# One fused transformer kernel: the last two weight chunks of each projection taken together, and convolution taps on 32x32 tiles of the matrix engine

## The reference, cut to what matters

```
mix = y @ w_out            # or: mix = act(conv(h @ w_up)) @ w_down
x = x + rmsnorm(mix, post_gain)
h = rmsnorm(x, pre_gain)   # input of the next half layer
```

```
u = h @ w_in + b_in                       # 1024 -> 2048
u = u[..., :D] * sigmoid(u[..., D:])
u = causal_dwconv(u, dw, dw_b)            # per channel: 31 taps over tokens
u = silu(layer_norm(u, ln_g, ln_b))
y = u @ w_out + b_out
```

## Time and profile before

| | us |
|---|---|
| median of 3 runs | 3412.98 |
| lowest, highest | 3412.93, 3414.3 |
| the profiled execution, its device time | 3412.23 |
| its span, first to last instruction | 3410.4 |
| PE busy | 3254.4 (95%) |
| DVE busy | 1780.0 (52%) |
| ACT busy | 1237.5 (36%) |
| POOL busy | 136.8 (4%) |

### The profile page before, as it was taken

The page is one execution under the profiler, slowest core; times in us unless marked ns, Lnnn a source line. Parts: engine busy times, 40 slices in busy tenths (PEclk is TensorE's granted clock), DMA queues, the critical chain, the costliest instruction groups (busy, mean ns, idle before and its releaser), DMA issues.

```text
span 3410.4 us, 41633 instructions
## 1 busy us (share of the span) xinstructions
PE 3254.4 (95%) x16677; PEld 2660.3 (78%) x16677; DVE 1780.0 (52%) x2348; ACT 1237.5 (36%) x1676; POOL 136.8 (4%) x148
## 2 busy tenths in 40 slices
PE   8899999999999899999999988999899999999999
PEld 7566888888877588888887657888788888888887
DVE  4655445553465734555527956553434424555543
ACT  3544224443334622444324234442322212243432
POOL 1130000000020300000000010000000000000000
PEclk9999999999999999999999999999999999999999
DMA  6221322322341123223232112223231221223322
GB/s 162 47 72 50 99 93 92 98 92 93 93 104 55 36 88 98 87 99 98 93 104 64 60 44 91 94 92 105 68 106 59 65 87 62 75 81 98 98 86 87
DMA packets 231696, 288.16 MB, mean 84 GB/s; under 512 B 5397, under 2 KB 188717, under 8 KB 231565
## 3 DMA queue, kind: packets, MB, share of 16 engines
q1 hardware_dynamic: 225628, 266.89, 24.2%
q0 software_dynamic: 5936, 19.40, 2.6%
HBM read 284.18 MB, written 2.10 MB: 84 GB/s over the span
## 4 chain that ended last, share of the span: by engine, by line
PE 86%; DVE 8%; ACT 3%; issue 3%; POOL 0%; DMA 0%; DVEq 0%; ACTq 0%; POOLq 0%
PE ps L1437 18%; PE ps L1439 18%; PE ps L1438 18%; PE ps L1553 6%; PE ps L1554 6%; PE ps L1555 6%; PE ps L1474 2%; PE ps L1476 2%; PE ps L1475 2%; PE ps L1813 2%; PE ps L1622 1%; ACT t_whi L588 1%; PE ps L1658 1%; DVE t_wlo L925 1%; PE ps L1907 1%
## 5 line engine op out<-in xcount | busy, mean ns | idle before, releaser
L925 DVE TENSOR_TENSOR t_wlo<-t_wraw,t_whi 128x2048 fp32r<-128x2048 f32 x252 | 582.4, 2311 | 1349.3 <-ACT t_whi L588 1349.3
L588 ACT ACTIVATE t_whi<-t_wraw 128x2048 fp32r<-128x2048 f32 x252 | 482.7, 1916 | 1498.3 <-PE ps L1439 1009.4
L1437 PE MATMUL ps<-t_hh,t_whi 128*128 128x512 f32 (+1 forms) x2640 | 988.9, 375 | 34.2 <-DVE t_hl L995 25.6
L1439 PE MATMUL ps<-t_hh,t_wlo 128*128 128x512 f32 (+1 forms) x2640 | 980.6, 371 | 0.0
L1438 PE MATMUL ps<-t_hl,t_whi 128*128 128x512 f32 (+1 forms) x2640 | 980.4, 371 | 0.0
L1437 PEld LDWEIGHTS ps<-t_hh,t_whi 128*128 128x128 f32 x2640 | 501.9, 190 | 125.9 <-issue 23.7
L1438 PEld LDWEIGHTS ps<-t_hl,t_whi 128*128 128x128 f32 x2640 | 501.7, 190 | 86.7 <-issue 2.9
L1439 PEld LDWEIGHTS ps<-t_hh,t_wlo 128*128 128x128 f32 x2640 | 501.5, 190 | 84.4
L1555 PE MATMUL ps<-t_whi,t_midl 128*128 128x512 f32 x704 | 273.9, 389 | 0.0
L1553 PE MATMUL ps<-t_whi,t_midh 128*128 128x512 f32 x704 | 273.9, 389 | 0.0
L1554 PE MATMUL ps<-t_wlo,t_midh 128*128 128x512 f32 x704 | 273.9, 389 | 0.0
(11 more groups left out here) (258 smaller groups left out, 3971.4 us busy)
## 6 DMA issues: line engine op xcount, KB each, us to landing
t_wraw<-in_w_in_dram SPq DMA_DIRECT2D x46, 1024.0 KB, 5.3
t_wraw<-in_w_up_dram SPq DMA_DIRECT2D x44, 1024.0 KB, 5.1
t_wraw<-in_ffn_w_in_dram SPq DMA_DIRECT2D x44, 1024.0 KB, 5.1
t_wraw<-in_w_kv_dram SPq DMA_DIRECT2D x24, 1024.0 KB, 5.2
t_wraw<-in_w_down_dram SPq DMA_DIRECT2D x20, 1024.0 KB, 5.0
t_wraw<-in_ffn_w_out_dram SPq DMA_DIRECT2D x20, 1024.0 KB, 5.0
t_wraw<-in_w_branch_dram SPq DMA_DIRECT2D x12, 1024.0 KB, 5.0
t_wraw<-in_w_q_dram SPq DMA_DIRECT2D x12, 1024.0 KB, 5.1
```

The source lines that it names most:

```text
L588: sc.activation(whi[slot][:, :], wraw[slot][:, :], ACT.Copy).then_inc(w_hi, 1)
L925: v.tensor_tensor(wlo[slot][:, :], wraw[slot][:, :], whi[slot][:, :].bitcast(F32), ALU.subtract).then_inc(w_lo, 1)
L1437: te.matmul(out, wh, xh, start=first, stop=False)
L1439: return te.matmul(out, wl, xh, start=False, stop=last)
```

## The change

Three things change.

**Last two chunks together** (`last_two`). PE takes tiles 0 and 1 of the last but one chunk, then tiles 0 and 1 of the last (complete now), then tiles 2 and 3 of the last but one, which frees that chunk; then it turns row 0, does tile 2 of the last chunk, turns row 1, does tile 3. So rows 0 and 1 are turned within the product and no longer in `first_two`. In the hand-over the preparation of the next stage's first chunk (`hi(c - 1)`, `lo(c - 1)`) stands after the first two rows, that of its second chunk (`hi(c)`, `lo(c)`) after `add_mix` of row 3. The table load for the square root moves ahead of the squares of the first half.

**First two chunks**: the second chunk's half for tiles 0 and 1 is split into its two row tiles, with both transposes (rows 2 and 3) between them. After down2 the list of its own only loses its first two transposes.

**Convolution taps**: DVE does 15 taps of tiles 0 to 5 and 11 of tiles 6 and 7; PE does the other 16 and 20. PE is used as 16 tiles of 32x32: row group i holds channels 32i to 32i+31, column group g takes taps g, g+4, ... and writes partitions 32g of bank i (`partial_taps`). ACT copies the four banks to `part` (`copy_partials`), PE adds the four groups with a stacked 128x32 identity (`join_taps`), DVE adds the result (`add_joined`). POOL makes the 32x32 diagonals and sums tiles 0 to 6 of `vb` into `usum`, so that PE needs two matmuls for the layer norm's mean.

```diff
-PE_TAPS = 10
+DVE_TAPS = (15, 15, 15, 11)
...
-            tapd = sb("tapd", 4 * PE_TAPS * P, stack=s)
+            tapd = [sb(f"tapd{i}", 20 * 32, stack=s) for i in range(2)]
+            part, usum, stack = sb("part", 8 * T, stack=s), sb("usum", T, stack=s), sb("stack", 32, stack=s)
...
+        def pe_taps(t):
+
+            return TAPS - DVE_TAPS[t // 2]
+
+        def part_bank(t, i):
+
+            return bank(4 + i) if t < KT - 1 else bank(i)
...
+            def tap_diagonals(t):
+
+                n = pe_taps(t)
+                if t >= 2:
+                    pool.wait_ge(tapped, t - 1)
+                r0 = ROWS["cm_dw_2"][0] + 8 * DVE_TAPS[t // 2] + t
+                w = pvec[:, r0:r0 + 8 * (n - 1) + 1:8].rearrange("p (n o) -> p n o", o=1).broadcast_to([P, n, 32])
+                eye = stack[:, :].rearrange("p (o m) -> p o m", o=1).broadcast_to([P, n, 32])
+                gp.tensor_tensor(tapd[t % 2][:, 0:32 * n].rearrange("p (n m) -> p n m", n=n), eye, w,
+                                 ALU.mult).then_inc(taps_in, 1)
+
+            pool.wait_ge(h_lo, SPLIT["pre4"] + 8)
+            pool.dma_start(stack[:, :], A["c_stack"]).then_inc(stack_in, 16)
+            pool.wait_ge(stack_in, 16)
+            tap_diagonals(0)
+            tap_diagonals(1)
+            for t in range(KT - 1):
+                if t + 2 < KT:
+                    tap_diagonals(t + 2)
+                pool.wait_ge(convolved, t + 1)
+                if t == 1:
+                    ins = gp.tensor_tensor(usum[:, :], tile(vb, 0), tile(vb, 1), ALU.add)
+                elif t > 1:
+                    ch.link(ins)
+                    ins = gp.tensor_tensor(usum[:, :], usum[:, :], tile(vb, t), ALU.add)
+            ins.then_inc(usum_done, 1)
...
             def hand_over(h, c):
 
                 pre = f"pre{h + 1}"
-                root_table()
                 post_root(h, c, 0)
                 post_root(h, c, 1)
                 pre_root(pre, 0)
                 pre_root(pre, 1)
-                post_root(h, c, 2)
+                hi(c - 1)
                 row_hi(pre, hh, 0)
                 row_hi(pre, hh, 1)
+                post_root(h, c, 2)
+                post_root(h, c, 3)
                 hi(c)
-                post_root(h, c, 3)
                 pre_root(pre, 2)
+                pre_root(pre, 3)
                 row_hi(pre, hh, 2)
-                pre_root(pre, 3)
                 row_hi(pre, hh, 3)
...
-            def tap_diagonals(j):
-
-                if j >= 2:
-                    act.wait_ge(tapped, 2 * (j - 1))
-                for m in range(2):
-                    t = 2 * j + m
-                    for i in range(PE_TAPS):
-                        at = ((t % 4) * PE_TAPS + i) * P
-                        ins = sc.activation(tapd[:, at:at + P], ident, ACT.Copy, scale=col("cm_dw_2", 8 * (TAPS - PE_TAPS + i) + t))
-                    ins.then_inc(taps_in, 1)
...
+            def copy_partials(t):
+
+                act.wait_ge(tapped, t + 1)
+                if t >= 2:
+                    act.wait_ge(joined, t - 1)
+                for i in range(4):
+                    sc.activation(tile(part, 4 * (t % 2) + i), part_bank(t, i), ACT.Copy).then_inc(part_out, 1)
 
             c = FIRST["cm_in"]
             for j in range(4):
+                if j:
+                    copy_partials(2 * j - 2)
                 hi(c + 2 * j)
+                if j:
+                    copy_partials(2 * j - 1)
                 hi(c + 2 * j + 1)
                 for m in range(2):
 
                     act.wait_ge(drained, 2 + DRAINS["cm_in"] + 2 * j)
                     sc.activation(tmp[m], cm_bank(j, 1, m), ACT.Sigmoid, bias=col("cm_b_in_2", 8 + 2 * j + m)).then_inc(u_sig, 1)
-                tap_diagonals(j)
+            copy_partials(KT - 2)
+            copy_partials(KT - 1)
...
                 add_mix(h, 1)
                 scale_row(pre, 0)
                 scale_row(pre, 1)
-                gain_rest(h, c, 2)
+                lo(c - 1)
                 row_lo(pre, hh, hl, 0)
                 row_lo(pre, hh, hl, 1)
-                lo(c)
+                gain_rest(h, c, 2)
                 add_mix(h, 2)
                 bias_rest(h, c, 3)
-                scale_row(pre, 2)
                 gain_rest(h, c, 3)
                 add_mix(h, 3)
+                lo(c)
+                scale_row(pre, 2)
+                scale_row(pre, 3)
                 row_lo(pre, hh, hl, 2)
-                scale_row(pre, 3)
                 row_lo(pre, hh, hl, 3)
...
+            def add_joined(t, done=None):
+
+                m = t % 2
+                ch.wait(last[m])
+                dve.wait_ge(joined, t + 1)
+                ins = v.tensor_tensor(tile(vb, t), tile(vb, t), part_bank(t, 0), ALU.add)
+                ins.then_inc(tap_added, 1)
+                dve.wait_ge(tap_added, t + 1)
+                if done:
+                    v.memset(small[:, 16:17], 0.0).then_inc(convolved, 1)
...
-                    add_tapped(j - 1)
+                    add_joined(2 * j - 1, True)
                 dve.wait_ge(u_ready, 2 * j + 2)
                 last = [0, 0]
-                for k in range(TAPS - PE_TAPS):
+                for k in range(DVE_TAPS[j]):
+                    if k == 12:
+                        add_joined(2 * j)
...
+                if j < 3:
+                    ch.wait(last[0])
+                    v.memset(small[:, 16:17], 0.0).then_inc(convolved, 1)
+            add_joined(KT - 2, True)
+            add_joined(KT - 1, True)
...
             def first_two(c, name):
 
-                turn_row(name, 0)
-                turn_row(name, 1)
                 pe.wait_ge(w_lo, c + 1)
                 pe.wait_ge(h_lo, SPLIT[name] + 4)
                 rows_half(c, (hh, hl), 0, 0)
+                pe.wait_ge(w_lo, c + 2)
+                row_half(c + 1, (hh, hl), 0, 0, bank(1))
                 turn_row(name, 2)
-                pe.wait_ge(w_lo, c + 2)
-                rows_half(c + 1, (hh, hl), 0, 1)
                 turn_row(name, 3)
+                row_half(c + 1, (hh, hl), 0, 1, bank(5))
                 pe.wait_ge(h_lo, SPLIT[name] + 8)
                 rows_half(c, (hh, hl), 1, 0).then_inc(w_used, 1)
                 rows_half(c + 1, (hh, hl), 1, 1).then_inc(w_used, 1)
...
+            def last_two(c, bufs, ka, kb, last, pre):
+
+                pe.wait_ge(w_lo, c + 1)
+                for b in range(2):
+                    token_tile(c, bufs, b, 1, ka, kb, last)
+                pe.wait_ge(w_lo, c + 2)
+                for b in range(2):
+                    token_tile(c + 1, bufs, b, 1, kb, last + 1, last).then_inc(mix_done, 1)
+                for b in range(2, 4):
+                    ins = token_tile(c, bufs, b, 1, ka, kb, last)
+                ins.then_inc(w_used, 1)
+                if pre:
+                    turn_row(pre, 0)
+                token_tile(c + 1, bufs, 2, 1, kb, last + 1, last).then_inc(mix_done, 1)
+                if pre:
+                    turn_row(pre, 1)
+                token_tile(c + 1, bufs, 3, 1, kb, last + 1, last).then_inc(w_used, 1)
...
-            def taps(j):
-
-                for m in range(2):
-                    t = 2 * j + m
-                    pe.wait_ge(taps_in, t + 1)
-                    pe.wait_ge(u_ready, t + 1)
-                    if j:
-                        pe.wait_ge(convolved, t - 1)
-                    for i in range(PE_TAPS):
-                        at, u0 = ((t % 4) * PE_TAPS + i) * P, t * UW + TAPS - PE_TAPS + i
-                        ins = te.matmul(bank(4 + m), tapd[:, at:at + P], ub[:, u0:u0 + T], start=i == 0, stop=i == PE_TAPS - 1)
-                    ins.then_inc(tapped, 1)
-
-            def ln_mean(j):
-
-                for t in (2 * j, 2 * j + 1):
-                    pe.wait_ge(convolved, t + 1)
-                    ins = te.matmul(bank(7), meanm, tile(vb, t), start=t == 0, stop=t == KT - 1)
-                if j == 3:
-                    ins.then_inc(summed, 1)
+            def partial_taps(t):
+
+                pe.wait_ge(taps_in, t + 1)
+                pe.wait_ge(u_ready, 2 * (t // 2) + 2)
+                if t and t < KT - 1:
+                    pe.wait_ge(tap_added, t)
+                n = pe_taps(t)
+                for r in range(n // 4):
+                    for i in range(4):
+                        for g in range(4):
+                            q, p = 4 * r + g, 32 * i
+                            u0 = t * UW + DVE_TAPS[t // 2] + q
+                            ins = te.matmul(part_bank(t, i)[32 * g:32 * g + 32, :], tapd[t % 2][p:p + 32, 32 * q:32 * q + 32],
+                                            ub[p:p + 32, u0:u0 + T], start=r == 0, stop=r == n // 4 - 1)
+                ins.then_inc(tapped, 1)
+
+            def join_taps(t):
+
+                pe.wait_ge(part_out, 4 * t + 4)
+                for i in range(4):
```

(28 more changed lines are left out.)

91 lines of the change are left out of this document (41 added, 50 removed).

## The result

| | time, us | runs |
|---|---|---|
| before | 3412.95 (3411.12 to 3414.30) | 4 |
| after | 3351.26 (3349.82 to 3351.89) | 4 |
| after / before | 0.9819, 95% interval 0.9802 to 0.9836 | |
| profiled execution after | 3351.72, span 3349.8 | 1 |

What follows compares the result with a forecast made beforehand. PE, busy 95% of the span, was taken as the bound, its work plus its waits. From 3412.2 us, 37 for hand-overs and 27 for the convolution gave 3348, or 3349 against the median; range 3338 to 3380.

Steps and rivals of the forecast that it cites:

- Hand-overs of the common kind: Five hand-overs like out0 and down0: last two chunks through `first_two` take 49.7 us against 54.5, 4.8 gained each, 24 together.
- no spare, 0.1 taken: Common hand-over: `lo(c)` ends on DVE at 29.9 us, just when PE ends the first chunk's half and wants it.
- Out2: Hand-over with bias add ahead of each square: 2.5 us waited for row 0, `lo(c)` 2.7 late; 54.9 against 60.6, 5.7 gained.
- Down2: Hand-over that keeps its 6.3 us wait, some 3 waited for rows 2 and 3: 63.3 against 71.1, 7.8 gained.
- A tile's taps: Convolution on PE: a tile's 128 records take 4.2 us near full overlap, 4.5 with two changes of array form.
- Issue: Rival in the convolution: eight tiles at once or 54 ns a pair, 7.0 us a tile, 24 back, 3373; chance 0.18.
- Passes that don't flow into each other: Rival in the convolution: passes with their ends make a tile's taps 5.2 us, 8.5 more, 3357; chance 0.2.
- The slower rival: Convolution: tiles overlap only four at a time, a tile's taps cost 13.7 + 0.35 us, 3430; chance 0.06.
- Copies of the partial sums: Convolution: ACT's clearing of four banks, 2.2 us, is covered by PE's 5.5 us row tile except behind the last pair.
- Three pairs: Convolution: PE sets 33.3 us a pair (matmuls 21.9, visits 9.0, joins 2.4), ending at 1934.8; DVE keeps up.
- Behind the last pair: End of convolution: PE waits 5 us, taps 2 x 5.6, copies 2.2, join 1.2; layer norm starts about 1959, not 1986.0.
- The clock falls: Sign against the forecast: the clock falls to 1.2 GHz in the convolution's stretches of small tiles.

Runs made afterwards that it cites:

- Experiment 8: Changed kernel with POOL's sums released later, warm-keeping matmuls, mean of tiles 6 and 7 on PE, and out2's rows 0 and 1 turned behind tile 2, last chunk earlier: 3352.42 us.
- experiments 5 and 6: Changed kernel with a tile's 64 tap matmuls reordered: one group of 32 rows after the other, 3408.83 us; one 32x32 tile after the other, 3816.54 us.
- Experiment 9: Changed kernel with POOL's tap matrices and sums started in DVE's wait for the second chunk's high part, mean of tiles 5, 6 and 7 on PE: 3345.05 us.
- Experiment 4: Changed kernel with seven unused matmuls in PE's waits: five ahead of tile 6's taps, one ahead of the last join, one ahead of the mean: 3349.33 us.
- 11: Changed kernel with POOL's work in DVE's wait, out2's rows 0 and 1 turned behind tile 2, last chunk earlier, unused matmuls also in the layer norm: 3340.01 us.
- experiment 7: Changed kernel with POOL's sums released by DVE two taps later (four for the second), beside the three-operand multiply-adds: 3359.93 us.

## Why the prediction was right

**The sum.** 64 us were forecast, 61.7 came. Two errors of opposite sign stand in it: the hand-overs gave 39 instead of 37, the convolution 22 instead of 27. The two kernels with one half each confirm the split (37.9 and 23.2). Luck has a part in the small miss. By the two traces these parts, 39.3 and 22.1, less the 2.8 us that out2's first chunk lost, make 58.6 of the 60.6 us between the spans. The other 2.0 lie in stretches that the change doesn't touch, 0.7 ahead of out0's product and 1.35 between down0 and out1, where traces of the same code differ by as much: that product starts between 491.0 and 492.8 us in the traces with the new hand-over.

**Hand-overs of the common kind: right, 5.4 instead of 4.8.** The clock of rows and chunks held. Row 0 and row 1 are waited for nowhere, the low parts neither, and the one place that had "no spare, 0.1 taken" is the one wait, 0.31 us. What was too dear is the turned row. It was set at 1.07, which is the time from its first start to its last end; in a stream two of them move the next product by 1.66 us (546.76 to 548.42), 0.83 each, since the ends lie over the next matmuls. Four rows make 1.0 us, from which the wait takes 0.2 more than was set.

**Out2: 3.8 instead of 5.7.** The waits are as forecast, 2.44 us for row 0 (2.5) and 2.52 for `lo(c)` (2.7). The step left out is what follows such a wait here: row 0 is turned at half clock (1.97 us instead of 1.04), tile 2 behind it takes 3.6 instead of 2.8, and the first 24 half matmuls behind the second wait 4.3 instead of 3.0. Experiment 8 exchanges both waits for four others of 4.3 us in all, and the clock stays at 1.00.

**Down2: 8.5, forecast 7.8.** The wait of 6.3 us stays, those for its rows are 1.69, 0.30 and 1.57, where some 3 were set.

**A tile's taps: right.** 4.47 us with filling, 4.5 with the changes of array form forecast. Issue is no limit: a start follows the last by 7 ns at first and by 17 later, not by 54. *Passes that don't flow into each other* (5.2 us) is out. The Trainium skill (TensorE: Matmul & The Clock Gate, Measured speedup vs the span model) has 10.6 times for sixteen such tiles packed once; the prediction carried that over to eight rounds in a row. For those it is 128 x 0.429 / 4.47 = 12.3 times, and the trace decides.

**The slower rival** didn't come, but its ground was real: experiments 5 and 6 show that the overlap of sixteen belongs to the order of the loops, not to the tiles.

**Copies of the partial sums: right.** They are covered at six visits; behind the last pair 1.16 us of them show. The rule of the Trainium skill that was weighed (TensorEngine Tiling, PSUM Bottleneck) costs nothing else here.

**Three pairs: 102.9 instead of 99.9 us.** This is the step that failed. The prediction summed DVE's loop with each operation at its price alone, and only `u` was set on a clock ("it fits by little"). That held: PE never waits for `u` in the three pairs. What it gave no time to is the sum of the joined taps, which DVE makes behind its twelfth tap and which PE wants before the taps of the next tile. POOL's new work (tap matrices and sums) was taken as free, since POOL is idle. It isn't free for DVE: the first tap of the second tile takes 1.50 instead of 0.54, a multiply-add beside a tap matrix 1.57 instead of 0.74. DVE comes late with that sum by 0.90 and 1.13 us:

```profile
1868.07 4.76 PE L1884 MATMUL ps<-t_ub,t_tapd 32*32 32x512 f32 x128 [0.90 <-DVE t_vb L1366]
```

These two waits are 2.0 of the 3.0 us. Experiment 9 moves POOL's work: the sum is there 1.0 us before PE wants it, both waits go, and the three pairs take 100.5 us. The Trainium skill (SBUF — State Buffer, SBUF: two separate sides) has a rule that would have given such a term: GpSimd, and a DVE operation in a mode with two ports or with two SBUF inputs (this only against a GpSimd operation that reads SBUF), share a pair of ports, and whichever starts first holds it for the whole instruction while the other is blocked. The trace agrees in the main: the tap that starts at 1850.43, beside a sum of POOL from 1850.13 to 1851.64, ends at 1851.93, 0.3 behind that sum; and a sum of POOL that starts beside DVE's `lo` takes 3.26 us, the 1.28 of its own and the 2 that `lo` had to go. That it is this pair of ports, and not another cause with the same times, no run here separates.

Nor does every operation of POOL beside the taps cost DVE something. In the first pair of the changed kernel it is POOL alone that pays, 11.85 us for a tap matrix of 1.07, and DVE's 22 multiply-adds take 14.66 us, as in experiment 9 without POOL beside them; in the second pair they take 15.47. POOL, then DVE in the first and the second pair:

```profile
1821.44 11.85 POOL L576 TENSOR_TENSOR t_tapd<-t_stack,t_pvec 128x512 f32<-128x512 f32 x1 [18.29 <-PE ps L1884]
```
```profile
1817.68 14.66 DVE L1405 SCALAR_TENSOR_TENSOR t_vb<-t_ub,t_pvec,t_vb 128x512 f32<-128x512 f32 x22
...
1851.85 15.47 DVE L1405 SCALAR_TENSOR_TENSOR t_vb<-t_ub,t_pvec,t_vb 128x512 f32<-128x512 f32 x22
```

What decides which of the two pays, the runs don't show.

**Behind the last pair: 26.1 instead of 24.2.** The wait of 5.3 us was forecast (5). Behind it the taps of two tiles take 12.5 us instead of 11.2 and the two means 3.5, at a granted clock of 0.84 and 0.55. "The clock falls" was named as what would make the forecast wrong, for the stretches of small tiles; those stay at 1.00, and it falls behind the wait of 5.3. Experiment 4 gives 1.6 us of it back.

**Out2's first chunks, 2.8 us more than before,** were in no term. They are a matter of the clock, 0.88 in that stretch against 1.00 before. The loss is there with the old convolution (2.5) and with the new one alone (1.6), stays when only the taps are kept warm (4), is 1.6 in experiment 9, and goes when more matmuls are put into the layer norm's own waits (11). That points at those waits, but doesn't show them as the cause: the kernel before has much the same waits and 1.00, and why was not tried.

## What to carry to other kernels

- Set a hand-over on a clock, step by step and engine by engine, and look for the place without spare: the whole gain hung on which of two lines ACT and DVE took first (3351 or 3434 us), and the one wait left was where the clock said.
- Where small tiles work at once, let consecutive matmuls go to different tiles; the same 64 matmuls took 4.5, 9.1 or 54 us by loop order alone.
- Work given to an idle engine isn't free for its neighbour on the critical path: put it where that one waits. Four operations of POOL in DVE's wait cost nothing; three beside its taps, in experiment 7, about 1 us each.
